# Moving a ring of weight slabs from 64 to 128 bytes (modulo 256) off the activations it is multiplied with, and the layers' output slabs to the ring that lies 0 bytes off

## The reference, cut to what matters

```python
x = x + 0.5 * _swiglu(_rmsnorm(x, ffn1_norm[l]), ffn1_w_gu[l], ffn1_w_down[l])      # width 5632
x = x + _token_mixing(_rmsnorm(x, mix_norm[l]), w_in[l], ..., w_out[l])             # 10788 columns in, three kinds of attention
x = x + 0.5 * _swiglu(_rmsnorm(x, ffn2_norm[l]), ffn2_w_gu[l], ffn2_w_down[l])
...
for l in range(2):                                                                  # the second block: two layers
    h = _rmsnorm_2(x, norm_g[l]) * (1.0 + scale[:, None, :]) + shift[:, None, :]
    z = h @ w_in[l]                                                                 # 2048 -> 13 * 512 columns
    ...                                                                             # Fourier, neighbourhood, retention, convolution
    y = jnp.concatenate([o_fft, o_na, o_ret, o_cv], axis=-1) @ w_out[l]
    x = x + gate[:, None, :] * y
return _rmsnorm_2(x, final_g)
```

## Time and profile before

| | |
|---|---|
| median of 3 runs | 3177.79 us (3175.86 to 3178.54) |
| the profiled execution: its own time | 3180.05 us |
| its span, from the first to the last instruction | 3177.9 us |
| PE busy | 3139.9 us, 99% |
| DVE, ACT, POOL busy | 1737.8 us, 1448.2 us, 1254.6 us |
| granted TensorE clock, mean | 0.997 of 2.4 GHz |

### The profile page before, as it was taken

The page is one execution under the profiler, slowest core; times in us unless marked ns, Lnnn a source line. Parts: engine busy times, 40 slices in busy tenths (PEclk is TensorE's granted clock), DMA queues, the critical chain, the costliest instruction groups (busy, mean ns, idle before and its releaser), DMA issues.

```text
span 3177.9 us, 46730 instructions
## 1 busy us (share of the span) xinstructions
PE 3139.9 (99%) x19210; PEld 2770.5 (87%) x19210; DVE 1737.8 (55%) x2374; ACT 1448.2 (46%) x1883; POOL 1254.6 (39%) x621
## 2 busy tenths in 40 slices
PE   8999999999999999999999999999999999999998
PEld 7888888888899999998888888888899998899986
DVE  4555555543223447775545455544469855588654
ACT  5444444444566445544544444444444444544344
POOL 4444444445466454476444444444610004510013
PEclk9999999999999999999999999999999999999999
DMA  7888888775686554455688888877675545764444
GB/s 237 272 266 259 263 265 264 262 256 183 191 181 173 144 154 133 126 151 201 220 269 264 260 265 265 264 264 259 181 192 171 159 132 194 175 197 155 149 157 164
DMA packets 490237, 662.35 MB, mean 208 GB/s; under 512 B 73624, under 2 KB 278152, under 8 KB 489768
## 3 DMA queue, kind: packets, MB, share of 16 engines
q1 hardware_dynamic: 484536, 653.62, 65.9%
q0 software_dynamic: 4448, 3.96, 0.5%
q10 hardware_dynamic: 1040, 1.78, 0.2%
HBM read 657.14 MB, written 2.10 MB: 207 GB/s over the span
## 4 chain that ended last, share of the span: by engine, by line
PE 97%; DVE 2%; ACT 1%; DMA 0%; issue 0%; POOL 0%; SPq 0%; DVEq 0%; ACTq 0%
PE ps L862 35%; PE ps L790 22%; PE ps L867 18%; PE ps L796 11%; PE ps L780 2%; PE ps L1092 1%; PE ps L1075 1%; PE ps L821 1%; PE ps L1314 1%; PE ps L917 1%; PE ps L1278 0%; PE ps L1034 0%; DMA x_res<-in_x 0%; DVE narrow_split_slabs L1785 0%; PE ps L1008 0%
## 5 line engine op out<-in xcount | busy, mean ns | idle before, releaser
L742 POOL TENSOR_TENSOR split_slabs<-stage,split_slabs 128x1024 fp32r<-128x1024 f32 x266 | 649.8, 2443 | 837.5 <-ACT split_slabs L1368 837.5
L1368 ACT ACTIVATE split_slabs<-stage 128x1024 fp32r<-128x1024 f32 x528 | 559.4, 1061 | 822.4 <-PE ps L867 813.2
L1368 ACT ACTIVATE narrow_split_slabs<-stage 128x1024 fp32r<-128x1024 f32 (+1 forms) x504 | 528.0, 1052 | 800.2 <-PE ps L796 590.7
L742 POOL TENSOR_TENSOR narrow_split_slabs<-stage,narrow_split_slabs 128x1024 fp32r<-128x1024 f32 (+1 forms) x211 | 510.9, 2428 | 929.5 <-ACT narrow_split_slabs L1368 929.1
L790 PE MATMUL ps<-h_split,narrow_split_slabs 128*128 128x256 f32 x5856 | 749.0, 281 | 1.3 <-ACT gn L1565 1.3
L790 PEld LDWEIGHTS ps<-h_split,narrow_split_slabs 128*128 128x128 f32 x5856 | 702.8, 188 | 18.7 <-issue 15.2
L1785 DVE TENSOR_TENSOR split_slabs<-stage,split_slabs 128x1024 fp32r<-128x1024 f32 x262 | 331.1, 1264 | 698.4 <-ACT split_slabs L1368 698.3
L862 PE MATMUL ps<-split_slabs,h_split 128*128 128x512 f32 x2816 | 700.1, 391 | 0.0
L862 PEld LDWEIGHTS ps<-split_slabs,h_split 128*128 128x128 f32 x2816 | 526.6, 188 | 107.7
L1785 DVE TENSOR_TENSOR narrow_split_slabs<-stage,narrow_split_slabs 128x1024 fp32r<-128x1024 f32 x293 | 374.3, 1280 | 279.5 <-ACT narrow_split_slabs L1368 278.6
L796 PE MATMUL ps<-h_split,narrow_split_slabs 128*128 128x256 f32 x2928 | 397.3, 278 | 1.4 <-POOL narrow_split_slabs L742 1.3
(11 more groups left out here) (245 smaller groups left out, 2391.1 us busy)
## 6 DMA issues: line engine op xcount, KB each, us to landing
stage<-in_w_in SPq DMA_DIRECT2D x360, 512.0 KB, 3.7
stage<-in_ffn_w_gu SPq DMA_DIRECT2D x352, 512.0 KB, 4.6
U<-in_w_ada SPq DMA_DIRECT2D x192, 512.0 KB, 5.6
stage<-in_ffn_w_down SPq DMA_DIRECT2D x176, 512.0 KB, 5.1
stage<-in_w_out SPq DMA_DIRECT2D x96, 512.0 KB, 4.2
stage<-in_w_in SPq DMA_DIRECT2D x80, 128.0 KB, 3.0
stage<-in_w_branch_c SPq DMA_DIRECT2D x32, 192.0 KB, 3.3
stage<-in_cmp_w SPq DMA_DIRECT2D x8, 512.0 KB, 6.0
```

What stands on the lines that cost most here:

```text
L742: nc.gpsimd.tensor_tensor(slab_part(n, 1, size(n)), stage[:, n % RING, 0:size(n)], slab_part(n, 0, size(n)).bitcast(F32), ALU.subtract).th ...
L1368: return fn(slab_part(n, 0, size(n)), stage[:, n % RING, 0:size(n)], ACT.Copy)
```

## The change

Three things change. `SHIFT` goes from 16 to 32 floats and `OSP` from 16 to 32. The addresses modulo 256, counted from `h_split`, become: `split_slabs` and `act_split` 0 as before, `narrow_split_slabs` 128, `merged_split` 128, `heads_split` 256, that is 0. And the output slabs of the two layers, 32 each, go into the places of `split_slabs` (its first three), in place of `narrow_split_slabs`. The moving operand then lies ahead of the stationary one by 128 in the narrow products with `h_split`, by 128 in those with `heads_split`, and by 0 in all wide products.

Each layer now goes through a change of ring twice, and `before[n]` is worked out for these too. At the head of the second layer slab 1 must wait for the last output slab of the first layer; ACT rounds it one step later, behind the norm (`round_upto(s0 + 1 - l)`).

```diff
-SHIFT = 16
+SHIFT = 32
...
-QK, VN, OSP = 0, 25 * S, 16
+QK, VN, OSP = 0, 25 * S, 32
...
+        out_slabs = {n for l in range(2) for n in range(S_LAY[l] + LAY_SLABS - 8 * OUTG, S_LAY[l] + LAY_SLABS)}
+        in_wide_ring = lambda n: n < S_MIX or S_F2 <= n < S_LAY[0] or n in out_slabs
...
-            if n in (S_F1, S_MIX, S_F2, S_LAY[0]):
+            if n in (S_F1, S_MIX, S_F2, S_LAY[0], min(out_slabs), S_LAY[1] + LAY_SLABS - 8 * OUTG):
                 _k = 0
...
-            if n in (S_MIX, S_F2, S_LAY[0]):
-                _old, _side = dict(_user), -1 if n == S_F2 else 1
+            if n > 0 and in_wide_ring(n) != in_wide_ring(_last):
+                _old, _side, _new = dict(_user), -1 if in_wide_ring(n) else 1, _k
             before[n] = _user.get(slot[n])
-            if n >= S_MIX and _k < ring_n:
+            if n >= S_MIX and _k < _new + ring_n:
                 before[n] = max(_old.get(slot[n], 0), _old.get(slot[n] + _side, 0))
...
         def slab_part(n, which, width=SLAB):
 
-            ffn = n < S_MIX or S_F2 <= n < S_LAY[0]
-            return (ws if ffn else narrow_ws)[:, slot[n], which, 0:width]
+            return (ws if in_wide_ring(n) else narrow_ws)[:, slot[n], which, 0:width]
...
             for l in range(2):
                 s0, g0 = S_LAY[l], G_LAY[l]
-                round_upto(s0 + 1)
+                round_upto(s0 + 1 - l)
```

More of the change, by code:

```diff
@@ L507, in build @@
                 before[n] = max(before[n], last_branch)
-            _user[slot[n]] = n
+            _user[slot[n]] = _last = n
             _k += 1
```

## The result

The changed kernel takes 3218.85 us (median of 4 runs, 3214.83 to 3222.16). The kernel before, run beside it, takes 3177.24 us (4 runs, 3175.86 to 3178.54). The ratio is 1.013, 95% interval 1.0113 to 1.0148. So it is 1.3% slower, and the predicted range ended at 3202 us. The profiled execution's own time is 3222.16 us, 42.1 us above that of the kernel before.

The account below looks back on a forecast made before the run. PE, busy for 99% of the span, was taken to bound the kernel. Gains of 16.1 + 2.6 + 1.7 = 20.4 us from the median of 3177.8 gave 3157.4, predicted as 3157.5 us, range 3151 to 3202 us.

Parts of the forecast that it names:

- Narrow products with `h_split`, -64 to 128: 9072 matmuls on PE, forecast all at the quick pace of 113.3 ns: gain 16.1 us.
- if all go at the slow pace, +24.2: Narrow products with `h_split`: loss of 24.2 us if all 9072 run at 117.8 ns.
- The share of slow matmuls, 0.4: Narrow products with `h_split` in the kernel before: 0.4 of them slow, 0.3 to 0.5 allowing for rounding.
- Branch products, -2.6 us: 576 narrow products with `heads_split`, +64 to 128: from slow to quick pace, gain 2.6 us.
- Output slabs, -1.7 us: Wide products of the layers' output stages, +64 to 0: 768 matmuls from 228.9 to 226.7 ns, gain 1.7 us.
- The seam between the layers: Slab 1 of layer 1 rounded behind the norm, low part and loads later: cost 0, at most 1 us.
- The feed-forward parts, 0: Feed-forward products, and `w_out` of the token mixing, keep offset 0: no change.
- Does the supply keep up?: Loads, roundings and low parts keep up with a quicker PE, as in layer 1 already: no term.
- 128 slow too: Rival: bad offsets form one arc with 128 its middle, all narrow streams slow: 3200 us, chance 0.24.
- Old mixture: Rival: restart moment behind transposes picks the pace, so only outputs, perhaps heads, gain: 3173.5 to 3176 us, chance 0.13.
- address without effect: Rival: the pace is a matter of timing alone, nothing changes: 3177.8 us, chance 0.08.
- Quicker than the quick pace: Rival: 113.3 ns is itself a collision that 128 could remove: at most 64 us more gain, chance 0.05.

Follow-up runs that it names:

- experiment 1: Kernel before with only the layers' output slabs moved to the wide ring, `SHIFT` and `OSP` left at 16: 3179.52 us, ratio 1.0002.
- experiment 2: Kernel before with only `SHIFT` and `OSP` set to 32, output slabs left in the narrow ring: 3217.06 us, ratio 1.0116.
- experiment 4: Kernel before with `SHIFT` and `OSP` at 0, every pair of operands 0 bytes apart modulo 256: 3225.06 us.
- experiment 5: Kernel of experiment 1 with output slabs' places counted from 2, so slab 1 of layer 1 is rounded ahead of the norm: 3181.28 us, ratio 1.0003.
- experiment 3: Kernel before with `SHIFT` and `OSP` at 48, so narrow products with `h_split` stand at +64 and branch products at -64: 3204.26 us.

## Why the prediction was wrong, step by step

**"Narrow products with `h_split`, -64 to 128 ... I take the quick one": this step failed.** It was put at -16.1 us; it is +31.9. The runs showed a mean of 118.67 ns at 128 in place of 115.15 at -64, in every stretch slower than the quick pace. Experiments 1 and 2 show that the distance makes the loss and the rings don't. Both reasons that I gave for the choice fell. 128 being "farthest from the operands' meeting" assumes that 0 is the bad place and the cost falls off with the distance: it does not, since -64 is better than 128, -96 and -32, and +32 better than +64. And "113.3 ns is what is left without a collision", taken from the equal ratio 17/16 of the wide products at 0, carried a finding from one kind of product to the other: experiment 4 has 119.9 ns for narrow and 227.2 ns for wide products at the same 0.

**The bound "if all go at the slow pace, +24.2"** was no bound. I took the two paces of the kernel before for the only two; the other distances have means of their own, from 116.8 to 119.9 ns, and 128 has 118.7 ns. That is 0.9 ns on 9072, 8 us more. I had given a pace slower than 117.8 ns a chance of 0.04 and no price. (The price itself was a slip: 117.8 - 113.3 is 4.5 ns, not 4.4, which makes 16.3 us of the 16.1 and changes nothing else.)

**The share of slow matmuls, 0.4:** right. From the distances it is (115.15 - 113.3)/4.5 = 0.41. But it belongs to one execution; in the second it is 0.51, just outside the 0.3 to 0.5 that I allowed.

**Branch products, -2.6 us:** the wrong sign, +0.5, from the same step.

**Output slabs, -1.7 us:** right, 226.7 ns, shown alone in experiment 1.

**"The seam between the layers ... All of it costs 0": wrong by about 2 us.** I asked when PE wants the slab and when ACT is free. Both answers hold. What I didn't ask is what else runs while POOL makes the low part: DVE's scalings, for which PE waits with nothing to do. Their six take 2.47 us without the low part beside them and 4.60 with it; experiments 1 and 5 differ in this and show it. POOL's issues of the bias loads, which run beside the scalings before, cost them nothing. The Trainium skill, page "SBUF — State Buffer", section "Who interferes with whom", has VectorE and GpSimd share a pair of ports that one instruction holds to its end; the trace agrees: the one scaling that met the low part of 2.56 us took 2.57 us and ended behind it, the others kept their 0.5 us.

**The head of the output stages, 0:** right, PE has no wait there in the profile after. **The feed-forward parts, 0:** about 1.1 us slower, for a reason that no run shows.

**"Does the supply keep up? ... No term":** the argument was for a quicker PE and PE got slower, so it was not tested. Still the supply failed at times, while the bias was loaded: 8.9 us in one profile of the changed kernel, 2.2 in another, between 0.3 and 3.8 in all others. The waits are not the change's, as far as two profiles of one kernel can tell. Why they are long in one execution was not found.

**The rule against the change.** By the Trainium skill, page "TensorE: Matmul & The Clock Gate", section "Part 2: What happens when you issue a matmul", the address would be worth nothing, as the two reads have ports of their own. The runs say otherwise: with the same instructions the distance moves the kernel between 3179 and 3225 us.

**The rivals.** "128 slow too" came nearest: it priced all narrow products at 117.8 ns, so 3200 us, and they ran at 118.7. It has the right sign for the wrong reason, since its mechanism, one arc of bad distances with 0 outside it, is refuted by experiment 4. "Old mixture" and "address without effect" fell with experiment 2. "Quicker than the quick pace" fell too: no distance gave a stretch below 113.3 ns. The upper end of the range, 3202 us, was owed to "128 slow too", and the time lies 17 us above it.

**Open.** Why narrow products want -64 and wide ones 0. No model of mine gives the table; what is shown is that the distance sets the pace within 0.7 ns and, at -64, within the two paces; how is not shown. For the narrow products both operands were moved together only by 128 bytes, between the kernel before and experiment 3. Nor is it known what makes a stretch at -64 quick or slow, beyond the program having most of it.

## What to carry to other kernels

The distance modulo 256 bytes between the moving and the stationary operand of fp32r matmuls is a parameter worth 1.4% here. Measure it in steps of 32 bytes for each shape of product; do not reason from one shape to another or from two points to a third. And when a step on POOL is moved, look at what DVE does at that moment, and not only at who waits for the step.

## What the runs showed of the hardware

- Matmuls of 256 columns follow each other at 113.3 to 120.0 ns and those of 512 columns at 226.7 to 233.6 ns, depending on that distance, at a full granted clock.
- At -64 the same program runs a stretch at 113.3 ns in one execution and at 117.8 in the next, though 80% of it keeps its pace. At 128 the mean was 118.7 ns in all five profiles.
- Behind waits of PE of 2.3 to 2.5 us the granted clock fell (0.57 in a window of 4 us), and 13 to 15 matmuls went at 213 ns. The wait of 2.5 us therefore cost 4.2.
- A scaling of 128x512 float32 on DVE takes 0.48 us, and 2.57 us when it meets POOL's low part of a slab, which takes 2.56 us. Beside POOL's issues of DMAs it keeps 0.48 us.
